# Hybrid Hyena/SSD trunk on one core: modulation pieces moved behind the Hyena projection's tiles

## The reference, cut to what matters

```python
def _adaln(cond, ada_w, ada_b):                    # cond: c_ctx for context, c for latent tokens
    m = jax.nn.silu(cond) @ ada_w + ada_b          # 1024 x 6144 for each layer
    return jnp.split(m[:, None, :], 6, axis=-1)    # sh1, sc1, g1, sh2, sc2, g2

xs = x_sample + sincos_2d(...)                     # positions, latent tokens only
for i in range(2):
    h = rmsnorm(x, norm_g[i, 0]) * (1 + sc1) + sh1
    x = x + g1 * mixer_i(h)
    h = rmsnorm(x, norm_g[i, 1]) * (1 + sc2) + sh2
    x = x + g2 * expert_choice_ffn(h)
```

## Time and profile before

| what | us |
|---|---|
| median of three runs | 4223.14 (4219.71 to 4225.56) |
| the profiled execution, its own time | 4222.11 |
| its span, first to last instruction | 4220.1 |
| opening (phase_modulation), from 0 | 125.3 |
| first norm | 54.8 |
| Hyena projection with its weights' arrival | 358.4 |
| long convolution | 440.2 |
| Hyena output | 129.4 |
| route of layer 0 / of layer 1 | 167.2 / 110.6 |
| experts of layer 0 / of layer 1 | 775 / 776 |

### The profile page before, as it was taken

The page is one execution under the profiler, slowest core; times in us unless marked ns, Lnnn a source line. Parts: engine busy times, 40 slices in busy tenths (PEclk is TensorE's granted clock), DMA queues, the critical chain, the costliest instruction groups (busy, mean ns, idle before and its releaser), DMA issues. The chain is left out here.

```text
span 4220.1 us, 56631 instructions
## 1 busy us (share of the span) xinstructions
PE 3665.0 (87%) x22647; PEld 2943.9 (70%) x22647; DVE 1829.6 (43%) x2961; ACT 1294.1 (31%) x2039; POOL 454.1 (11%) x419
## 2 busy tenths in 40 slices
PE   8499979896788999999599999558999579999995
PEld 1399934345527999999499999435555469999995
DVE  3433345553342333333420355478888433333332
ACT  0323320201222223322421333325665323222332
POOL 0000000000011211112000011230000011121111
PEclk9699979798888999999799999779999589999997
DMA  7422130105575887888232222777665648888875
GB/s 247 161 68 60 35 112 26 42 22 172 221 280 205 299 296 277 290 291 300 72 108 92 63 85 68 247 286 274 221 223 191 235 162 288 293 300 281 291 281 180
DMA packets 384017, 806.39 MB, mean 191 GB/s; under 512 B 21636, under 2 KB 66428, under 8 KB 382466
## 3 DMA queue, kind: packets, MB, share of 16 engines
q1 hardware_dynamic: 346012, 707.40, 47.3%
q0 software_dynamic: 29184, 91.16, 7.3%
q10 hardware_dynamic: 8719, 6.51, 0.5%
HBM read 691.29 MB, written 113.71 MB: 191 GB/s over the span
## 5 line engine op out<-in xcount | busy, mean ns | idle before, releaser
L1647 PE MATMUL moe_banks<-moe_xt,mix_ring 128*128 128x144 f32 x8192 | 1012.6, 287 | 3.1 <-ACT moe_xt L1682 3.1
L1647 PEld LDWEIGHTS moe_banks<-moe_xt,mix_ring 128*128 128x128 f32 x8192 | 1011.3, 191 | 5.5 <-issue 3.2
L62 PE MATMUL ssdin_banks<-h_leading,ssdin_w_split 128*128 128x384 f32 x1920 | 385.3, 334 | 5.8 <-ACT ssdin_pad L1943 2.9
L1669 PE MATMUL moe_banks<-moe_down_parts,moe_hid_parts 128*128 128x512 f32 x1536 | 357.5, 392 | 0.0
L62 PEld LDWEIGHTS ssdin_banks<-h_leading,ssdin_w_split 128*128 128x128 f32 x1920 | 337.1, 188 | 7.2 <-issue 7.2
L1669 PEld LDWEIGHTS moe_banks<-moe_down_parts,moe_hid_parts 128*128 128x128 f32 x1536 | 285.9, 188 | 71.4 <-issue 13.2
L1727 DVE TENSOR_TENSOR moe_hid<-moe_banks,moe_sg 128x128 f32<-128x128 f32 x256 | 74.7, 292 | 580.5 <-ACT moe_sg L1705 580.5
L1717 DVE TENSOR_TENSOR moe_down_parts<-mix_ring,moe_down_parts 128x2048 fp32r<-128x2048 f32 x128 | 292.3, 2284 | 0.0
L1614 POOL DMA_INDIRECT x_dram<-moe_yc,mix_idx_quarter x128 | 167.6, 1309 | 1088.7 <-DVE moe_yc L1738 1059.4
L2495 PE MATMUL scan_banks<-scan_w,scan_yc 128*128 128x512 f32 x576 | 257.5, 601 | 0.0
L62 PE MATMUL hyin_banks<-h_leading,hyin_w_split 128*128 128x384 f32 x1152 | 236.6, 340 | 19.5 <-DVE hyin_w_split L575 19.2
(11 more groups left out here) (333 smaller groups left out, 4646.0 us busy)
## 6 DMA issues: line engine op xcount, KB each, us to landing
mix_ring<-in_moe_w_gate SPq DMA_DIRECT2D x64, 2048.0 KB
mix_ring<-in_moe_w_up SPq DMA_DIRECT2D x64, 2048.0 KB, 12.9
mix_ring<-in_moe_w_down SPq DMA_DIRECT2D x64, 2048.0 KB, 8.6
scan_cum<-row_dram SPq DMA_DIRECT2D x36, 1024.0 KB
mod_w<-in_ada_w SPq DMA_DIRECT2D x12, 2048.0 KB, 8.1
mix_ring<-in_ada_w SPq DMA_DIRECT2D x12, 2048.0 KB, 15.5
ssdin_w<-in_ssd_in_w SPq DMA_DIRECT2D x10, 2048.0 KB, 9.7
scan_states<-s_dram SPq DMA_DIRECT2D x36, 512.0 KB, 7.8
```

Of the source, the lines that this page charges most:

```text
L62: ins = pe.matmul(out(piece), w_at(w[a], k), h_k(h[b], k, piece), start=(k == 0 and a == 0 and b == 0), stop=(k == KD - 1 and a == 1))
L1647: ins = pe.matmul(pb[:, 2 * (f % 2) + j, 0:SLOTS], ring[:, 2 * half + j, k, col:col + P], xt[:, k, :], start=(k == 0), stop=(k == KD - 1))
L1669: ins = pe.matmul(pb[:, LAT_BANK[half], :], hid_parts[:, a, k, :], wd[:, half, b, k, :], start=(k == 0 and a + b == 0), stop=(k == KD - 1 ...
```

## The change

- The opening and the first norm become one phase, `phase_front`. It computes four pieces of layer 0 (shift and scale of the first norm). The piece's store is one 2 MB buffer in four quarters; a quarter is reloaded when its products are done.
- Each product is column-tiled: `cond_t` is padded to 32 columns, and four products of 128 weight columns write to partitions 0, 32, 64 and 96 of a bank. The sum lies as 128 x 128, a row of it for each 128 columns at 32j (context) and 32j+1 (latent). The bias rows are laid out alike; a plain 128 x 128 transpose turns them.
- The remaining eight pieces of layer 0 and all twelve of layer 1 are computed in `phase_hyena_in`, one after each of the first twenty tiles, into the unused 128 columns of the tile's own bank. The tile's eviction on ACT waits for the piece's add on DVE. Rows for the gates and the second norm are stored from there to `vec_dram`; the first four pieces of layer 1 are transposed there too.
- `phase_hyena_in` is written out, no loop; its weights come through a ring of three single tiles, three of them loaded in the opening. u of a block is transposed right after the block's third tile (and the ninth part after the next tile), not in pairs of blocks.
- The filter network works on 128 partitions x 1152 in place of 64 x 2304; `w3` is loaded twice, once for each half of the partitions.
- The norm no longer stores x; `phase_hyena_out` loads inputs and positions again and adds them. Rings in the opening are 3 (x) and 2 (positions).
- Parameter and bias loads go from ACT's queue to POOL's. `NextModulation` is removed from `phase_route`.

The core of the diff:

```diff
+    def load(self, sp, n):
+        layer, at = n // 12, n % 12 * HALF
+        for u in range(ADA_SLOTS):
+            if n:
+                sp.wait_ge(self.s_acc, ADA_SLOTS * (n - 1) + u + 1)
+            sp.dma_start(self.ring[:, u, :, :], self.ada[:, layer, u, :, at:at + HALF]).then_inc(self.s_in[u], 16)
+    def product(self, pe, n, out):
+        for u in range(ADA_SLOTS):
+            pe.wait_ge(self.s_in[u], 16 * (n + 1))
+            for k in range(ADA_K):
+                for j in range(4):
+                    ins = pe.matmul(out[32 * j:32 * j + 32, :], self.keep["cond_t"][:, u * ADA_K + k, :],
+                                    self.ring[:, u, k, j * P:(j + 1) * P],
+                                    start=(u == 0 and k == 0), stop=(u == ADA_SLOTS - 1 and k == ADA_K - 1))
+            ins.then_inc(self.s_acc, 1)
...
+                mod.load(sp, 0)
                 filt.load(sp)
...
+                for n in range(1, FRONT_PIECES):
+                    mod.load(sp, n)
+                for t in range(TILES):
+                    b = t % RING
+                    if t >= RING:
+                        sp.wait_ge(s_xn, t - RING + 1)
+                    sp.dma_start(xr[:, b, :], src(t)).then_inc(s_x[b], 16)
+                    if t:
+                        if t >= 3:
+                            sp.wait_ge(s_add, t - 2)
+                        sp.dma_start(pos[:, t % 2, :], io["pos"][(t - 1) * P:t * P, :]).then_inc(s_pos[t % 2], 16)
+                for q in range(3):
+                    hyena_weights(sp, io, keep, q)
+                mod.load(sp, FRONT_PIECES)
...
+                mod.product(pe, 0, pb[:, PIECE_BANK[0], 0:P])
+                filt.products(pe, pb, 0)
                 pe.wait_ge(s_stage, 16 * (len(keep["param_rows"]) + 2))
...
+                mod.product(pe, 1, pb[:, PIECE_BANK[1], 0:P])
+                filt.products(pe, pb, 1)
+                mod.product(pe, 2, pb[:, PIECE_BANK[2], 0:P])
+                mod.product(pe, 3, pb[:, PIECE_BANK[3], 0:P])
+                pe.wait_ge(s_row, FRONT_PIECES)
+                for n in range(FRONT_PIECES):
+                    ins = pe.transpose(pb[:, MOD_BANK, n * P:(n + 1) * P], rows[:, n, :], keep["ident"][:, :])
+                ins.then_inc(s_mt, 1)
```

and in `phase_hyena_in`:

```diff
+                for q in range(HY_TILES):
+                    if q + 3 < HY_TILES:
+                        sp.wait_ge(s_lo, q + 1)
+                        hyena_weights(sp, io, keep, q + 3)
+                    if q + 1 < LAST:
+                        mod.load(sp, q + 1 + FRONT_PIECES)
+                    if q == FIRST_1 + 1:
+                        vectors(0)
+                    if q == LAST + 1:
+                        vectors(1)
...
+                for q in range(HY_TILES):
+                    project(q)
+                    turn_piece(q)
+                    if q < LAST:
+                        mod.product(pe, q + FRONT_PIECES, piece_out(q))
+                    if q % 3 == 2:
+                        turn(q // 3, (0, 1))
+                    if q and q % 3 == 0:
+                        turn(q // 3 - 1, (2,))
+                turn(HY_TILES // 3 - 1, (2,))
...
+                def evict(q):
+                    if q < LAST:
+                        act.wait_ge(s_row, q + 1)
+                    else:
+                        act.wait_ge(s_mm, q + 1)
```

More of the change, by code:

```diff
@@ new lines, in tile_evict @@
+                def tile_evict(t):
+                    act.wait_ge(s_xt, t + 1)
+                    if t == 0:
+                        act.wait_ge(s_gain, 4)
+                    if t >= 2:
+                        act.wait_ge(s_lo, t - 1)
+                    for k in range(0, 4):
+                        gain, shift = args(t, k)
+                        act.activation(hf[:, t % 2, k, :], pb[:, 2 * (t % 2) + k // 4, (k % 4) * P:(k % 4 + 1) * P],
+                                       ACT.Identity, bias=shift, scale=gain).then_inc(s_ea, 1)
@@ L188, in _ @@
                 pe.wait_ge(s_c, 32)
-                pe.transpose(pb[:, 0, 0:16], cond_rows[:, :], keep["ident"][0:16, 0:16]).then_inc(s_ct, 1)
+                pe.transpose(pb[:, 7, 0:16], cond_rows[:, :], keep["ident"][0:16, 0:16]).then_inc(s_ct, 1)
                 pe.wait_ge(s_silu, 2)
[L191 to L203, removed]
@@ L443, in phase_hyena_in @@
         pb = m.psum()
-        s_w = [m.sem(f"w_in{b}") for b in range(2)]
         s_hi = m.sem("w_leading")
@@ new lines, in vectors @@
+                def vectors(layer):
+                    at = 12 * layer
+                    sp.wait_ge(s_row, 12 * (layer + 1) - FRONT_PIECES)
+                    sp.wait_ge(s_ar, 2 * layer + 2)
+                    for which, n in ((V_G1, 4), (V_B2, 6), (V_A2, 8), (V_G2, 10)):
+                        for c in range(2):
+                            sp.dma_start(row_blocks(io["vec_dram"][layer, c, which]), rows[c::32, at + n:at + n + 2, :]
+                                         ).then_inc(s_vec, 16)
@@ new lines, in turn_piece, with turn @@
+                def turn_piece(q):
+                    n = turned_piece(q)
+                    if n is not None:
+                        pe.transpose(turned_out(q), rows[:, 12 + n, :], keep["ident"][:, :])
+                def turn(blk, gos):
+                    b = blk % 2
+                    pe.wait_ge(s_u, blk + 1)
+                    for go in gos:
+                        if blk or go == 2:
+                            pe.wait_ge(s_ur, 3 * blk if go < 2 else 3 * blk + 1)
+                        for t in range(*((0, 4), (4, 8), (8, 9))[go]):
@@ L529, in lead @@
[L529 to L543 removed]
+                                   bias=prm[:, 2, 96 + part * 8 + blk:97 + part * 8 + blk],
@@ L560, in _ @@
-                act.wait_ge(s_zero, 6)
-                with act.Fori(0, 3) as i:
-                    tiles(i, False)
-                tiles(3, True)
+                lead(0)
+                lead(1)
+                act.wait_ge(s_zero, 6)
+                for q in range(HY_TILES):
+                    evict(q)
+                    if q + 2 < HY_TILES:
+                        lead(q + 2)
+                    if q % 3 == 2:
+                        evict_u(q // 3, (0, 1))
+                    if q and q % 3 == 0:
+                        evict_u(q // 3 - 1, (2,))
@@ L639 @@
 class Filter:
-    BANKS = (4, 5, 6, 7, 0)
-    pieces = [(a, min(HALF, TAPS - a)) for a in range(0, TAPS, HALF)]
+    PIECES = 3
+    WIDTH = FOLD // PIECES
     def __init__(self, m, io, filt):
@@ L1299, in phase_route @@
         pb = m.psum()
-        nxt = None if layer else NextModulation(m, io, keep, pb)
         s_vec = m.sem("vectors_in")
```

692 lines of the change are left out of this document (343 added, 349 removed).

## The result

The changed kernel takes 4110.93 us (median; 4109.68 to 4113.13) against 4223.15 us before on the same chip: a ratio of 0.9735, 95% interval 0.9719 to 0.9752. It is faster and inside the range of 4070 to 4130, but 23 us slower than the 4088 predicted, and so outside the narrower 4070 to 4105 that the forecast gave itself 0.62 for. The profiled executions say the same: 4110.46 us (span 4108.8) against 4222.11, a gain of 111.65 where the sum gave 135.2.

A forecast was written before the change was run, and what follows sets the result against it. TensorE, busy for 87% of the span, was taken to bound the kernel, each stage having its own limit. The terms summed to -135.2 us, giving 4088 against the median 4223.1, range 4070 to 4130 for 8 in 10.

The forecast's parts named there:

- the eight terms: Opening -88.7, norm 0, projection start -7.6, projection +16.6, convolution +1.1, Hyena output 0, first route -56.6, everything behind 0 us.
- Removing products and DRAM round trip from the first route: First route: only the second route's work is left, so 167.17 us becomes 110.59, -56.6 us.
- The twenty pieces: Projection: twenty modulation pieces computed behind tiles cost 2.0 us each, +40 us; bounds +35 and +75.
- the transposes: Projection: pauses of 29.0 us for transposing u go, block-by-block transposes and layer 1 rows cost some back; -20.9 us.
- the reload: Projection: a piece's quarter reload has 12.5 us where 8.1 is the median, so it stays hidden by about 4 us.
- The first, an issue floor of 54.5 ns: Projection pieces: issue binds at 54.5 ns a record, 3.75 us a piece, 35 us more, 4123 us; chance 0.18.
- The third: Projection pieces: column tiles do not overlap in this form, 7.0 us a piece, +100 us, 4188; chance 0.04.
- fourth: Projection: slower than before, TensorE waiting for piece reloads at every product; loses from a landing of 19.3 us; chance 0.03.
- the fifth: Whole kernel: nothing measurable, the opening's gain eaten by pieces at a lower clock; chance 0.01.
- The second: Opening longer, or norm loads late: 10 to 25 us more, 4098 to 4113; chance 0.12 for the part beyond 4105.
- the first add after 55: Opening: first norm add later than 55 us, named as the sign that the longer-opening rival holds.
- the opening's -88.7: Opening: eight of twelve pieces leave, so the first norm add moves from 132.7 to 44 us; bounds 37 to 54.

The follow-up runs named there:

- experiment 9: Changed kernel with the 64 records of each of the projection's twenty pieces issued twice, the second set into unused columns; 4142.86 us, ratio 0.9807 to the kernel before.
- experiment 10: Changed kernel with 58 of the 64 records of each projection piece writing one position of 32 array columns instead of four; 4199.47 us, ratio 0.9947.
- experiment 11: Changed kernel with only 14 of the 64 records of each projection piece computed; 4091.60 us, ratio 0.9688 to the kernel before.
- experiment 12: Kernel before with the projection's loop written out and u transposed block by block, no pieces in it; 4205.57 us, ratio 0.9956.
- experiment 1: Changed kernel with the two d_skip loads issued from ACT's queue instead of POOL's; 4114.41 us, ratio 0.9735 to the kernel before.
- experiment 4: Changed kernel with the two d_skip loads moved out of the opening and issued by POOL in the convolution; 4094.85 us, ratio 0.9698 to the kernel before.
- experiment 7: Changed kernel with d_skip loaded on POOL's queue as one load of 32 adjacent values per partition, taken apart in SBUF; 4093.19 us, ratio 0.9696.
- experiment 8: Changed kernel with d_skip as one adjacent load, plus piece 1 ahead of the parameter transposes and piece 2 ahead of the filter's second layer; 4090.28 us, ratio 0.9689.
- experiment 3: Kernel before with only its d_skip loads moved from ACT's queue to POOL's; 4236.08 us, ratio 1.0028.
- experiment 6: Kernel before with its d_skip loads issued by POOL in the convolution; 4218.79 us, ratio 0.9989.

## Why the prediction was right, and where it failed

**Right.** The bound of each stage, and five of the eight terms to within 1.5 us. Removing products and DRAM round trip from the first route (-56.8 for -56.6) rested on reading a twin stage in the same trace, and came out within 0.2 us. The twenty pieces cost about 40 for 40 (experiments 9 to 12), with a burst of 1.88 where 1.75 was forecast and 0.1 beside it where 0.25 was; the transposes gave about 20 for 20.9 (experiment 12), and the reload stayed behind the tiles. That column tiles overlap was read from the experts' burst, and it holds for four tiles of 128 columns.

**Rivals.** The first, an issue floor of 54.5 ns, is false (28 ns). With it goes the estimate of 4.0 us a piece from the Trainium skill (TensorE: Matmul & The Clock Gate, "Wait — 56ns, not 53.3ns?"), which puts decode in microcode at about 62 ns a matmul. The section says so only for hardware decode off, a condition that the prediction left out; no run here shows which way decode went. A record comes every 28 to 29 ns here, and even a whole product of two records takes only 56 to 59. The third and fourth are false (experiment 10; no wait of TensorE for a piece in the projection), and so is the fifth: the clock was 0.98 over the projection. The second came true in its number, the first add after 55, and only in part in its cause.

**The step that failed** is the opening's -88.7, mis-sized by 21.0. The sentence was "POOL now issues the ten parameter loads and four bias loads that ACT issued; only piece 1 and the row adds wait for them." It counts who waits for the loads and not what they do to the transfers of the other queues. The two `d_skip` loads are among its ten, taken as equal to the rest. They took 17 to 20 us to land, and while they did almost nothing else moved. The Trainium skill has the rule that I did not apply (DMA: Bandwidth & Descriptors, "Rules for kernel authors"): a strided last dimension becomes one descriptor per element, and one should rearrange it. The 2080 packets of experiment 1 for 2048 elements agree. That section does not say what it costs. The worth of them here: 16 to 18 us of time (experiments 4 and 7). The other 3 us were the relay of pieces: my estimate was that piece 1 "fits in between" and that piece 2 runs at 28. In TensorE's order piece 1 stands behind the parameter transposes and piece 2 behind the filter's second layer, so that without the block (experiment 7) they began at 22.86 and 33.39. With the order changed the add came at 44.29 for a forecast of 44 (experiment 8). That the agreement is so close is partly luck: the filter's inputs were at 17.09 there, where I had allowed for 12.5.

The range held the result because the second rival, a longer opening (4098 to 4113), was in it. It had 0.12 for what lies beyond 4105. The lower bound, 4070, was never near.

**Open.** Why 4-byte elements cost this much, and whether by element or by partition, was not tried. Nor was the +3.3 in the convolution or the +3.6 behind the route taken apart; the prediction had said that more than 2 us in either would be outside its account, and only the spread between executions speaks for chance.

## What to carry to other kernels

When a step of loads is moved or put on another queue, list every transfer in it by number of elements, not bytes: one strided load of separate four-byte values can hold up the other transfers, whoever waits for it. Fetch the values adjacent and take them apart on chip. From POOL's queue the mark of it is a long idle stretch with a high DMA share and almost no GB/s. From ACT's queue the share stays low (2.4%); there the marks are thousands of tiny packets and long issues on other queues.

## What was not expected of the hardware

- 2048 elements of four bytes (8 KB) took 17 to 20 us to land (medians of 16.9, 18.7, 19.5 and 20.2 in experiments 4 and 3, the changed kernel and experiment 1). From POOL's queue they are 32 packets of mostly 7.3 to 9.4 us, sixteen at a time, and the other queues moved almost no data (0 to 5 GB/s from 13.6 to 25 us); from ACT's they are some 100 packets a microsecond, with 2.4% of the engines' time, and SP's issues took four times as long (8.38 for 1.94 us).
- 128-column fp32 records in four column positions run at 28 to 29 ns each and at 101 ns in a single one.
- The same load on ACT's queue cost the old opening 4 to 6.4 us (experiment 6) and the new one as much as on POOL's (experiment 1, no gain), where taking it away is worth 16 to 18. A likely reason is that the new opening has SP's small loads and the piece relay on its path, and that the loads stood first on ACT's queue in experiment 1; neither was tried by itself.
